# Retention heads: decay tables fetched ahead of the projections, and each head's scores issued ahead of the previous head's sums

## The chip, the cores and the metric

The kernel runs on one core of one Trainium2 chip, as one program with one launch. The metric is device time in microseconds, the median of several executions. All data is float32. The engines are TensorE (PE in the profile), VectorE (DVE), ScalarE (ACT), GpSimd (POOL) and SyncE (SP), which here only issues DMAs.

## The reference

Two blocks in a row act on 256 tokens of width 1024. The first block has an even layer (attention and a gated scan), an odd layer (retention), each followed by a feed-forward part; the second block has two layers with a gated delta rule and window attention. The change touches the odd layer's retention alone. It has 4 heads; queries and keys have 256 features each, values and gates 512. For the latent tokens:

```
p  = split_parts(h_lat @ w_in, ODD_PARTS)          # q, k, v, g
q_l = apply_rope(to_heads(p['q'], RET_HEADS), cos, sin)
k_l = apply_rope(to_heads(p['k'], RET_HEADS), cos, sin) * k_scale
v_l = to_heads(p['v'], RET_HEADS)
o_fw, _ = retention_chunked(q_l, k_l, v_l, log_g_fw, s_fw)
o_bw, _ = retention_chunked(flip(q_l), flip(k_l), flip(v_l), log_g_bw, s_bw)
y_lat = gated_head_norm(o_fw + flip(o_bw), p['g']) @ w_out
```

`s_fw` and `s_bw` come from the 256 context tokens. Retention is a product of queries and keys, weighted by a power of the head's decay that depends on the distance alone, times the values. `gated_head_norm` divides by the root mean square over the 512 values of a head and multiplies by silu of the gate.

## The kernel before

Every engine has its own hand-written order of instructions, and semaphores tie them together. Context and latent tokens (512 together) are kept as columns of `hT`. The kernel treats both directions and the context state of retention as one weighted score matrix for each head: 512 source tokens (four tiles of 128) by 256 target tokens. The weights are a table of 512 KB for each head, `const_ret[h]`, made on the host, and fetched into `r_D[:, h % 2]`, so there is room for two.

The odd layer runs in this order on TensorE: the norm; 8 blocks of query features, 8 of key features, 16 tiles of values and 8 of gates (`by_feature`, `by_token`, L775 and L763), whose weights come through a ring of two tiles of 2 MB that SyncE fills (L616) as TensorE releases them; then the four heads (L1277 to L1293); then transposes (`transposed`, L821) and the output projection (`down`, L805). ScalarE evicts each projection from a PSUM bank (`evac`, L1496), and VectorE sums modulation weights (L2106) in between and rotates queries and keys (L2632 to L2635).

For one head TensorE makes the scores into two PSUM banks, `mx[:, 0]` and `mx[:, 1]` (L1283: 8 matmuls of 256 columns), each bank signalled by `ret_s`. VectorE multiplies each bank by its half of the table into `r_P` (L2647, 2 instructions, signalled by `ret_p`). TensorE multiplies `r_P` with the values into banks `mx[:, 2]` and `mx[:, 3]` (L1291: 8 matmuls of 512 columns, signalled by `ret_o`). ScalarE squares and sums each of these banks (L1892, writing the squares to `r_junk`, which nobody reads), takes the logarithm and the exponential (L1550, L1551, signalled by `ret_rs`), and VectorE multiplies the bank, the reciprocal root and the gate (L2653, signalled by `ret_n`). Behind head h ScalarE waits for `ret_p` and issues the table of head h + 2 (`table`, L1868). Tables 0 and 1 are issued behind the last gate eviction (L1885, L1886).

The waits that hold the heads together: the scores of head h need both banks read (`ret_p`), the sums of head h need `r_P` written (`ret_p`) and their bank read (`ret_n`), VectorE's multiplication needs the table (`dtab_in`), the scores, and for h >= 2 the sums of head h - 2 (`ret_o`, since `r_P` has two halves).

`gate` is a buffer of 2 x 1024 columns that the norms use as scratch for squares and the reciprocal root (`n_sum`, `n_sq`, `n_rs`). `hT` holds the normed input, and from the transposes on (`roT`) the heads' outputs. `silu_tanh` and `exp_ln` load ScalarE's function tables (L1546, L1543).

Of the kernel before, what the change touches and what calls it, by code (L numbers as in the profile page):

```python
# [26 lines left out]
RET = 4  # L27
# [300 lines left out]
def need(eng, sem, value):  # L328

    if isinstance(value, int) and value <= 0:  # L330
        return
    eng.wait_ge(sem, value)
# [31 lines left out]
def first_then_second_block(nc, a, out):  # L364
# [3 lines left out]
    with ExitStack() as ctx:  # L368
        def sb(name, shape, dt=F32):
            return ctx.enter_context(nc.sbuf_tensor(name, shape, dt))  # L370
# [8 lines left out]
        gate = sb("gate", [P, 2, D])  # L379
# [16 lines left out]
        def view(at, *shape):  # L396
            n = int(np.prod(shape))
            assert at + n <= ARENA, (at, shape)
            v = arena[:, at:at + n]
            if len(shape) == 1:  # L400
                return v
            names = "abcd"[:len(shape)]
            return v.rearrange(f"p ({' '.join(names)}) -> p {' '.join(names)}", **dict(zip(names, shape)))
# [57 lines left out]
        hflat = hT[:, :, :].rearrange("p a b -> p (a b)")  # L461
# [33 lines left out]

        rv, rg, rk, rq = view(0, 4, 2048), view(8192, 2, 2048), view(12288, 8, 512), view(16384, 8, 256)
        r_t = view(18432, 2, 2, 256)
        r_P, r_D, r_junk = view(19456, 2, 4, 256), view(21504, 2, 4, 256), gate[:, 0, 0:512]

        dnf = view(0, 24, 256)  # L500
        sqk, s_v = view(6144, 2, 1152), view(8448, 2, 128)
# [193 lines left out]
        def _(pe):  # L695
# [39 lines left out]
            def bank():  # L735

                n = job.next()
                if pl.before[n] is not None:
                    emptied(pl.before[n] + 1, pl.who[pl.before[n]])
                return acc[:, pl.bank[n], :]  # L740

            def done(stage, n):

                emptied(pl.own[name_of(stage)][n - 1] + 1, pl.who[pl.own[name_of(stage)][n - 1]])
# [137 lines left out]
            def attention(base, units, fill):  # L882

                n = len(units)
                for u in range(n + 3):
                    if u < n:
                        q, k, blocks, v = units[u]
                        since(pe, att_m, base, u - 1)
                        nc.tensor.matmul(mx[:, u % 2, 0:P * blocks], q, k, start=True, stop=True).then_inc(att_s, 1)  # L889
                    fill(u)  # L890
                    if 2 <= u <= n + 1:
                        o, blocks = u - 2, units[u - 2][2]
                        pe.wait_ge(att_p, base + o + 1)
                        since(pe, att_pt, base, o)
                        for j in range(blocks):
                            ins = nc.tensor.transpose(mx[:, 2, P * j:P * (j + 1)], att_S[o % 3][:, P * j:P * (j + 1)], ident)
                        ins.then_inc(att_t, 1)
                    if u >= 3:
                        o, (_, _, blocks, v) = u - 3, units[u - 3]
                        pe.wait_ge(att_pt, base + o + 1)  # L900
                        since(pe, att_d, base, o)
                        for j in range(blocks):
                            ins = nc.tensor.matmul(mx[:, 3, HD * (o % 8):HD * (o % 8 + 1)],
                                                   att_PT[o % 2][:, P * j:P * (j + 1)], v[j],
                                                   start=j == 0, stop=j == blocks - 1)
                        ins.then_inc(att_o, 1)
# [21 lines left out]
            for i in BOTH:  # L928
                pe.wait_ge(qk_ready, i + 1)
                b = bank()  # L930
# [3 lines left out]
                b = bank()  # L934
# [84 lines left out]
            for slot in range(SLOTS):  # L1019
# [24 lines left out]
                if 3 <= slot < UNITS + 3:  # L1044
                    o, (_, _, blocks, v) = slot - 3, units[slot - 3]
                    pe.wait_ge(att_pt, o + 1)
                    since(pe, att_d, 0, o)
                    for j in range(blocks):
                        ins = nc.tensor.matmul(mx[:, 3, HD * (o % 8):HD * (o % 8 + 1)], ePT[o % 2][:, P * j:P * (j + 1)], v[j],
                                               start=j == 0, stop=j == blocks - 1)  # L1050
                    ins.then_inc(att_o, 1)
# [222 lines left out]
                by_token(tok, 512, where="odd")  # L1274
            pe.wait_ge(mod_c, len(MOD_GROUPS))
            done("ret_v", 16)
            for h in range(RET):  # L1277
                pe.wait_ge(ret_rope, h + 1)
                for s2 in range(2):
                    need(pe, ret_p, 2 * h - 1 + s2)  # L1280
                    for s in (2 * s2, 2 * s2 + 1):
                        for k in range(2):
                            ins = nc.tensor.matmul(mx[:, s2, 256 * (s % 2):256 * (s % 2) + 256],  # L1283
                                                   rk[:, 2 * h + k, P * s:P * (s + 1)], rq[:, 2 * h + k, :],
                                                   start=k == 0, stop=k == 1)
                    ins.then_inc(ret_s, 1)
                pe.wait_ge(ret_p, 2 * h + 2)
                for t in range(2):
                    need(pe, ret_n, 2 * h - 1 + t)
                    for s in range(4):  # L1290
                        ins = nc.tensor.matmul(mx[:, 2 + t, :], r_P[:, h % 2, s, P * t:P * (t + 1)],  # L1291
                                               rv[:, s, 512 * h:512 * (h + 1)], start=s == 0, stop=s == 3)
                    ins.then_inc(ret_o, 1)  # L1293
# [11 lines left out]
            for l in range(DEPTH2):  # L1305
# [12 lines left out]
                for i in range(2):  # L1318
                    pe.wait_ge(qk_ready, l * 2 + (NT + i + 1))
                    for j2 in range(2):  # L1320
                        b = bank()
# [4 lines left out]
                    b = bank()  # L1326
# [133 lines left out]
        def _(act):  # L1460
# [73 lines left out]
            def mod_after(where):  # L1534

                job_ = own.next()
                if job_ - 1 in MOD_SUM_AFTER.get(where, ()):
                    mod_turn()
                if job_ in MOD_SUM_AFTER.get(where, ()):
                    mod_sum()  # L1540

            def exp_ln():
                nc.scalar.preload_act_table_set(EXP_LN)  # L1543
# [323 lines left out]
            def table(h):  # L1867
                act.dma_start(r_D[:, h % 2], a["const_ret"][h]).then_inc(dtab_in[h % 2], 16)  # L1868

            own.n = 0  # L1870
            for f in range(8):
                evac(rq[:, f, :], 256)
# [8 lines left out]
            for c in range(4):  # L1881
                for t in range(2):
                    evac(rg[:, t, 512 * c:512 * (c + 1)], 512, ACT.Silu)
                    mod_after("odd")
            table(0)  # L1885
            table(1)  # L1886
            exp_ln()
            for h in range(RET):
                for t in range(2):
# [175 lines left out]
        def _(dve):  # L2065
# [5 lines left out]
            def name_of(stage):  # L2071

                return stage if layer[0] is None else f"{stage}@{layer[0]}"

            def job_done(name, n):

                dve.wait_ge(acc_a, pl.emptied("A", pl.own[name_of(name)][n - 1] + 1))
# [550 lines left out]
            for h in range(RET):  # L2628
# [8 lines left out]
                        link(ins)  # L2637
                ins.then_inc(ret_rope, 1)
                dve.wait_ge(ret_rope, h + 1)
            job_done("ret_g", 8)  # L2640
            for h in range(RET):
                dve.wait_ge(dtab_in[h % 2], 16 * (h // 2 + 1))
                if h >= 2:
                    dve.wait_ge(ret_o, 2 * (h - 1))
                for s2 in range(2):
                    dve.wait_ge(ret_s, 2 * h + s2 + 1)
                    V.tensor_tensor(r_P[:, h % 2, 2 * s2:2 * s2 + 2, :], mx[:, s2, :].rearrange("p (s t) -> p s t", s=2),  # L2647
                                    r_D[:, h % 2, 2 * s2:2 * s2 + 2, :], ALU.mult).then_inc(ret_p, 1)
                for t in range(2):
                    n = 2 * h + t  # L2650
                    dve.wait_ge(ret_rs, n + 1)
                    g = rg[:, t, 512 * h:512 * (h + 1)]
                    V.scalar_tensor_tensor(g, mx[:, 2 + t, :], st[:, 408 + n:409 + n], g,  # L2653
                                           ALU.mult, ALU.mult).then_inc(ret_n, 1)
# [15 lines left out]
            for l in range(DEPTH2):  # L2670
# [155 lines left out]
                for n in range(4):  # L2826
                    h, t = n // 2, n % 2
# [31 lines left out]
```

## Time and profile before

| | |
|---|---|
| median of 3 runs | 2884.79 us |
| lowest, highest | 2884.76, 2913.66 us |
| the profiled execution's own time | 2885.55 us |
| its span, first to last instruction | 2883.4 us |
| mean granted TensorE clock | 0.969 |
| TensorE busy | 2720.8 us, 94% |
| VectorE busy | 1542.3 us, 53% |
| ScalarE busy | 669.5 us, 23% |

The span is what the trace covers, and the time of an execution lies 2.15 us above it. Busy shares are averages over all stages. The profile shows each float32 matmul call as two records, so "x16" is eight calls of the source. A granted clock of 1.00 is 2.4 GHz and 0.50 is 1.2 GHz.

### The profile page before, as it was taken

The numbers are of one execution on the slowest core, as the hardware profiler recorded it, in microseconds if no ns is written. First come the engines' busy times: TensorE is split into PE (matmuls) and PEld (weight loads), VectorE is DVE, ScalarE is ACT, GpSimd is POOL, SyncE is SP. The second block draws the span as 40 slices with busy tenths as digits, with TensorE's granted clock in tenths as the row PEclk, the third lists the DMA queues.
The fourth block names the chain that finished last, engine by engine and source line by source line (L and its number), as shares of the span: only waits on it lengthen the run. The fifth ranks groups of instructions, "written<-read, shape, count | busy, mean of one in ns | idle before, by whom it ended". The sixth has DMA issues, their size and how long they took to land.

```text
span 2883.4 us, 36232 instructions
## 1 busy us (share of the span) xinstructions
PE 2720.8 (94%) x14426; PEld 2050.3 (71%) x14426; DVE 1542.3 (53%) x3100; ACT 669.5 (23%) x1727; POOL 0.2 (0%) x4
## 2 busy tenths in 40 slices
PE   6899988999999999899999999989998999998999
PEld 2445555888887444589977756668996864775999
DVE  4856555755775521136745554425773654443775
ACT  3134322111102100212111351222311144222330
POOL 0000000000000000000000000000000000000000
PEclk9998889999999999999999999999999999999999
DMA  7530012555475844145634221124553322113554
GB/s 291 200 94 23 34 55 88 175 161 171 174 282 199 304 165 163 59 130 164 181 131 151 97 88 59 59 88 130 164 182 127 134 88 88 59 59 101 154 168 134
DMA packets 336164, 387.36 MB, mean 134 GB/s; under 512 B 10988, under 2 KB 265084, under 8 KB 323452
## 3 DMA queue, kind: packets, MB, share of 16 engines
q1 hardware_dynamic: 333260, 378.15, 39.9%
q10 hardware_dynamic: 2736, 6.89, 0.7%
q8 instruction: 115, 1.88, 0.3%
q14 instruction: 53, 0.43, 0.0%
HBM read 383.96 MB, written 1.05 MB: 134 GB/s over the span
## 4 chain that ended last, share of the span: by engine, by line
PE 86%; DVE 6%; DMA 3%; ACT 3%; issue 2%; ACTq 0%; SPq 0%; DVEq 0%
PE acc L724 24%; PE acc L763 12%; PE acc L775 11%; PE mx L724 10%; PE acc L789 8%; PE acc L1031 2%; PE acc L1016 2%; PE acc L805 2%; PE mx L1409 1%; PE mx L1398 1%; PE mx L1407 1%; DVE arena L2106 1%; PE mx L889 1%; PE mx L1291 1%; PE acc L821 1%
## 5 line engine op out<-in xcount | busy, mean ns | idle before, releaser
L763 PE MATMUL acc<-ring,hT 128*128 128x512 f32 (+2 forms) x1152 | 407.6, 515 | 19.3 <-DMA ring<-in_even_w_in 9.5
L763 PEld LDWEIGHTS acc<-ring,hT 128*128 128x128 f32 x1152 | 197.9, 194 | 226.2 <-issue 207.6
L724 PE MATMUL acc<-arena 128*128 128x128 f32 (+1 forms) x2056 | 322.6, 299 | 2.1 <-ACT gate L1817 0.8
L775 PE MATMUL acc<-hT,ring 128*128 128x256 f32 (+1 forms) x1280 | 311.5, 407 | 12.8 <-DMA ring<-in_w_in 8.1
L775 PEld LDWEIGHTS acc<-hT,ring 128*128 128x128 f32 x1280 | 246.9, 193 | 76.5 <-issue 33.8
L724 PEld LDWEIGHTS acc<-arena 128*128 128x128 f32 x2056 | 282.8, 192 | 16.1 <-ACT gate L1817 1.4
L2106 DVE SCALAR_TENSOR_TENSOR arena<-mod_w,vcols,arena 128x2048 f32<-128x2048 f32 x98 | 228.4, 2348 | 110.4 <-DMA mod_w<-in_w_ada 100.9
L789 PE MATMUL acc<-ring,hT 128*128 128x512 f32 x512 | 258.0, 625 | 1.1 <-ACT hT L1496 1.1
L724 PE MATMUL acc<-hT,ring 128*128 128x128 f32 (+1 forms) x1208 | 194.9, 311 | 12.1 <-ACT hT L1586 12.0
L2453 DVE TENSOR_TENSOR arena<-ring 128x512 f32<-128x512 f32 (+1 forms) x136 | 91.6, 674 | 192.6 <-PE acc L724 184.7
L724 PEld LDWEIGHTS acc<-hT,ring 128*128 128x128 f32 x1208 | 171.6, 197 | 26.5 <-issue 11.8
L724 PE MATMUL acc<-arena,ring 128*128 128x128 f32 (+1 forms) x1160 | 182.4, 300 | 1.9 <-DVE x L2594 1.9
L724 PEld LDWEIGHTS acc<-arena,ring 128*128 128x128 f32 x1160 | 159.7, 192 | 10.4 <-DVE x L2594 2.7
L1496 ACT ACTIVATE arena<-acc 128x512 f32<-128x512 f32 (+2 forms) x136 | 69.8, 527 | 414.2 <-PE acc L763 293.4
L789 PEld LDWEIGHTS acc<-ring,hT 128*128 128x128 f32 x512 | 91.4, 196 | 89.7 <-issue 84.4
L724 PE MATMUL mx<-hT,ring 128*128 128x128 f32 (+1 forms) x928 | 151.0, 307 | 0.0
L724 PE MATMUL mx<-arena,ring 128*128 128x128 f32 (+1 forms) x928 | 148.5, 302 | 0.0
L724 PEld LDWEIGHTS mx<-hT,ring 128*128 128x128 f32 x928 | 132.5, 196 | 6.5
L724 PEld LDWEIGHTS mx<-arena,ring 128*128 128x128 f32 x928 | 128.7, 191 | 9.0 <-issue 3.4
L724 PE MATMUL acc<-hT,arena 128*128 128x128 f32 (+1 forms) x760 | 124.7, 307 | 0.0
L724 PEld LDWEIGHTS acc<-hT,arena 128*128 128x128 f32 x760 | 108.3, 191 | 6.0
L1031 PE MATMUL acc<-hT,ring 128*128 128x512 f32 x192 | 99.7, 659 | 0.0
(355 smaller groups left out, 3441.0 us busy)
## 6 DMA issues: line engine op xcount, KB each, us to landing
ring<-in_w_in SPq DMA_DIRECT2D x28, 2048.0 KB
mod_w<-in_w_ada SPq DMA_DIRECT2D x48, 1024.0 KB, 5.9
ring<-in_ffn_w_in SPq DMA_DIRECT2D x88, 512.0 KB
ring<-in_w_up SPq DMA_DIRECT2D x88, 512.0 KB
mod_w<-in_mod_w SPq DMA_DIRECT2D x40, 1024.0 KB, 5.0
ring<-in_odd_w_in SPq DMA_DIRECT2D x12, 2048.0 KB
ring<-in_ffn_w_out SPq DMA_DIRECT2D x16, 1024.0 KB
ring<-in_w_down SPq DMA_DIRECT2D x16, 1024.0 KB
```

Of the source, the lines that this page charges most:

```text
L724: ins = nc.tensor.matmul(out, w[:, k, :], h[:, k, :], start=start and k == 0, stop=stop and k == n - 1, skip_group_check=more)
L763: ins = nc.tensor.matmul(b[:, 0:width], src[:, k, P * i:P * (i + 1)], w[:, k, :], start=k == 0, stop=k == KD - 1)
L775: ins = nc.tensor.matmul(b[:, 0:hi - lo], w[:, k, P * f:P * (f + 1)], hT[:, k, lo:hi], start=k == 0, stop=k == KD - 1)
L789: ins = nc.tensor.matmul(filling.b, src[:, k, P * i:P * (i + 1)], filling.w[:, k, :], start=k == 0, stop=k == KD - 1)
L805: ins = nc.tensor.matmul(b[:, 0:width], w[:, k, P * f:P * (f + 1)], src[:, at + k, :], start=at + k == 0, stop=at + k == sum(groups) - 1)
L821: ins = nc.tensor.transpose(b[:, at:at + P], src[:, i, P * (k + q):P * (k + q + 1)], ident)
L889: nc.tensor.matmul(mx[:, u % 2, 0:P * blocks], q, k, start=True, stop=True).then_inc(att_s, 1)
L1016: ins = nc.tensor.matmul(b, w[:, k, P * f:P * (f + 1)], hT[:, first + k, :], start=k == 0, stop=k == 3)
L1031: ins = nc.tensor.matmul(hb, hw[:, kk, P * j:P * (j + 1)], hT[:, kk, :], start=kk == 0, stop=kk == KD - 1)
L1496: ins = nc.scalar.activation(dst, src, func, **kw)
L2106: ins = V.scalar_tensor_tensor(acc_, mod_w[:, i % 2, :], vcols[:, at:at + 1], acc_, ALU.mult, ALU.add)
L2453: V.tensor_tensor(s3, a11, a10, ALU.subtract)
```

## The change

Tables 0 and 1 are issued on ScalarE's queue before the first eviction of the odd layer's projections. The tables' place moves from the arena, where modulation sums live until the heads begin, to all of `gate`; `r_junk` moves from `gate` to the first 512 columns of `hT`. On TensorE the scores of head h + 1 are issued ahead of the sums of head h, and on VectorE the multiplication of head h + 1 ahead of the norm products of head h.

```diff
-        r_P, r_D, r_junk = view(19456, 2, 4, 256), view(21504, 2, 4, 256), gate[:, 0, 0:512]
+        r_P, r_junk = view(19456, 2, 4, 256), hflat[:, 0:512]
+        r_D = gate[:, :, :].rearrange("p a b -> p (a b)").rearrange("p (h s t) -> p h s t", h=2, s=4)
...
-            for h in range(RET):
+            def ret_scores(h):
                 pe.wait_ge(ret_rope, h + 1)
                 for s2 in range(2):
                     need(pe, ret_p, 2 * h - 1 + s2)
...
                     ins.then_inc(ret_s, 1)
+
+            ret_scores(0)
+            for h in range(RET):
+                if h + 1 < RET:
+                    ret_scores(h + 1)
                 pe.wait_ge(ret_p, 2 * h + 2)
...
             def table(h):
                 act.dma_start(r_D[:, h % 2], a["const_ret"][h]).then_inc(dtab_in[h % 2], 16)
 
+            table(0)
+            table(1)
             own.n = 0
...
-            table(0)
-            table(1)
             exp_ln()
...
-            job_done("ret_g", 8)
-            for h in range(RET):
+            def weighted(h):
                 dve.wait_ge(dtab_in[h % 2], 16 * (h // 2 + 1))
                 if h >= 2:
                     dve.wait_ge(ret_o, 2 * (h - 1))
...
+
+            job_done("ret_g", 8)
+            weighted(0)
+            for h in range(RET):
+                if h + 1 < RET:
+                    weighted(h + 1)
                 for t in range(2):
                     n = 2 * h + t
                     dve.wait_ge(ret_rs, n + 1)
```

## Rows read from the trace of the kernel before

**Rows 1.** The page: busy times, and the chain by engine.

```profile
PE 2720.8 (94%) x14426; PEld 2050.3 (71%) x14426; DVE 1542.3 (53%) x3100; ACT 669.5 (23%) x1727; POOL 0.2 (0%) x4
...
PE 86%; DVE 6%; DMA 3%; ACT 3%; issue 2%; ACTq 0%; SPq 0%; DVEq 0%
```

**Rows 2.** The chain of waits, retention heads: start us, length us, what.

```profile
1161.25 5.21 DMA arena<-in_const_ret
...
1166.65 1.30 DVE arena L2647 x2
...
1168.00 8.83 PE mx L1291 x16
1176.83 3.47 PE mx L1283 x16
...
1180.32 0.70 DVE arena L2647
...
1181.06 7.13 PE mx L1291 x16
...
1203.81 7.15 PE mx L1291 x16
...
1213.07 4.52 PE acc L821 x24
```

**Rows 3.** Timeline at the start of head 0: start us, us, what, idle before.

```profile
1161.53 3.72 PE L1283 MATMUL mx<-arena 128*128 128x256 f32 x16 [0.32 <-ACT modc L1522]
```

**Rows 4.** Windows: engines' busy us, then granted clock, DMA share, GB/s.

```profile
1165.00:1168.00 3.00, 0.26 (x3) 0.00 (x1) 1.29 (x2) 0.00 (x0) 0.00 (x0) 1.00 1.04 393
1169.40:1172.80 3.40, 3.40 (x6) 1.32 (x5) 0.00 (x0) 0.00 (x0) 0.00 (x0) 0.50 0.41 129
1173.00:1204.00 31.00, 28.65 (x90) 16.56 (x89) 8.37 (x12) 7.11 (x24) 0.00 (x0) 1.00 0.11 34
...
1213.80:1217.20 3.40, 3.40 (x19) 3.40 (x18) 0.00 (x0) 2.57 (x5) 0.00 (x0) 0.50 0.00 0
...
908.00:920.00 12.00, 12.00 (x52) 10.36 (x52) 5.30 (x4) 4.10 (x9) 0.00 (x0) 0.92 0.00 0
```

**Rows 5.** The line that issues the tables (L1868): time from issue to landing.

```profile
DMA to landing us min/median/max: 3.5/4.4/7.0
```

**Rows 6.** SyncE's queue: issues merged, from the first to the last.

```profile
895.11 26.51 SPq L616 DMA_DIRECT2D ring<-in_odd_w_in  x2
921.67 15.24 SPq L598 DMA_DIRECT2D mod_w<-in_w_ada  x4
...
1160.86 72.93 SPq L616 DMA_DIRECT2D ring<-in_odd_w_out  x2
```

**Rows 7.** Timeline, ScalarE at the projections' start, and at the tables' old place.

```profile
909.69 1.28 ACT L1546 ACT_TABLE_LOAD   x1
910.98 0.38 ACT L1496 ACTIVATE arena<-acc 128x256 f32<-128x256 f32 x1
914.26 0.38 ACT L1496 ACTIVATE arena<-acc 128x256 f32<-128x256 f32 x1 [2.90 <-PE acc L775]
...
1161.25 0.34 ACTq L1868 DMA_DIRECT2D arena<-in_const_ret  x1
```

**Rows 8.** Timeline behind the sums of head 0: table 2, and the norm product.

```profile
1177.91 0.34 ACTq L1868 DMA_DIRECT2D arena<-in_const_ret  x1
1178.14 0.75 DVE L2653 SCALAR_TENSOR_TENSOR arena<-mx,st,arena 128x512 f32<-128x512 f32 x1 [2.68 <-ACT st L1551]
```

**Rows 9.** The chain of waits, layers 0 and 1 of the second block.

```profile
1621.81 3.49 PE acc L763 x32
...
1905.51 3.69 PE acc L821 x16
...
2318.58 3.49 PE acc L763 x32
...
2598.79 2.95 PE acc L821 x16
```

## The prediction

> **What bounds the kernel now.** I began with the page. TensorE is busy for 94% of the span and holds 86% of the chain that ended last [rows 1], so an edit is worth what it takes off TensorE's own timeline. The change touches one stage, the retention heads. In the chain of waits of that stage [rows 2] the reader should see four heads, each a block of score products (3.47 us) and a block of weighted sums (7.13 us), and three kinds of lost time. First, in head 0, the chain leaves TensorE for a DMA: the decay table is issued at 1161.25 and takes 5.21 us. The timeline [rows 3] says that the scores of head 0 start at 1161.53, so they end at 1161.53 + 3.47 = 1165.00, and the sums start at 1168.00: **3.00 us** idle. Second, the sums of head 0 take 8.83 us where every later head takes 7.13 us, **1.70 us** more. The windows [rows 4] say why: from 1165 to 1168 TensorE is nearly idle, and from 1169.4 to 1172.8 its granted clock is 0.50, the 1.2 GHz level, against 1.00 (2.4 GHz) before the idle time. Third, in each later head the scores end at 1176.83 + 3.47 = 1180.30 and the sums start at 1181.06, after VectorE's second multiplication by the table (0.70): **0.76 us**, three times; these short gaps leave the clock at 1.00 [rows 4].
>
> **The change, part by part.**
>
> *Tables early.* Tables 0 and 1 are issued ahead of the projections' evictions instead of behind them. VectorE then never waits for them, as some 250 us lie between. Without the new order head 0 would still wait the ordinary 0.76, so this part removes 3.00 - 0.76 = 2.24 us, and with the long idle time the slow clock behind it, 1.70: **3.94 us**.
>
> What it costs. The two issues move to where ScalarE has loaded its function table, at 910.98, ahead of its first eviction [rows 7]. At their old place the first took 0.34 and the next began 0.37 after it, so the eviction comes under 1 us late. The next eviction waits 2.90 us for TensorE anyway, and TensorE fills four banks in turn, so it asks for the first again only four blocks (some 14 us) on. If that cover were gone the cost would be that one microsecond. On the DMA engines, the two transfers (1 MB together) fall into a stretch with nothing in it: from 908 to 920 their share is 0.00 [rows 4]. SyncE issued its first projection load of [rows 6] at 895.11, and then waited until 921.2 to issue the second, because the ring had to be released; nothing of it is queued behind ScalarE. Issued at about 911 with the longest landing seen (7.0 us, [rows 5]) they are in by 918.4 and meet nothing. Cost: zero, and at worst, were they to collide with a weight load that TensorE waits for, the 2.7 us that 1.05 MB takes at the 393 GB/s of [rows 4].
>
> The Trainium skill speaks against this part (DMA: Bandwidth & Descriptors, "Issuing engines are not separate DMA queues"): loads started by ScalarE run on the same 16 DMA engines as SyncE's and interleave with them. Read that way, an early fetch only moves 1 MB into another load's time. The trace bears the rule out at the old place, where tables and an output weight tile are in flight together and the first table takes 5.21 us against 3.5 for the undisturbed ones; at the new place there is no other load, so the sum stays.
>
> *New places.* The decay tables move into the norm's scratch, and the square's throw-away output into the start of hT. Both are the same SBUF accesses at other addresses: zero. The norm's next writer of that scratch comes after all heads, and hT's last reader, the last gate projection, is ahead of the heads on TensorE. No wait is added by either.
>
> *Scores one head ahead.* TensorE's order becomes S0, S1, W0, S2, W1, S3, W2, W3 (S scores, W sums). VectorE multiplies head h+1 ahead of the norm products of head h. Nothing is added, the same instructions run. Step by step from 1161.53, with 3.47 and 7.13: S0 ends at 1165.00. S1's first half needs bank 0, read by VectorE after S0's first half (1163.27 + 0.70 = 1164.0): free. Its second half, due 1166.74, needs the second multiplication: 1165.00 + 0.76 = 1165.8: free. S1 ends at 1168.47, and W0 has had its factors since 1165.8. W0 to 1175.60, S2 to 1179.07, W1 to 1186.20, S3 to 1189.67, W2 to 1196.80, W3 to **1203.93**. The banks of the sums are free in time too: the norm product is done some 2.1 us after a half of the sums (1210.96 to 1213.07 for the last), so the first bank is free for W3 at 1196.80 - 3.57 + 2.1 = 1195.3, 1.5 us ahead, and the second at 1198.9 for 1200.4; W1 and W2 have more. In the trace W3 ends at 1203.81 + 7.15 = 1210.96. The new order takes 4 x 0.76 = 3.04 us, the tables 3.94, together 6.98; the two end points give 7.03. I take **7.0 us**.
>
> The new order's cover for tables 2 and 3: ScalarE issues a table 1.08 us after a head's sums (1177.91 against the end at 1176.83, [rows 8]), so table 2 at 1176.7 and table 3 at 1187.3. Before, table 2 was wanted when head 2's first scores were done, from about 1189.8, 12 us after its issue. Now table 2 must be in before S3 wants bank 0 at 1186.2, less 0.7: 8.8 us. Table 3 must be in early enough for its two multiplications (1.35) and the norm product of head 2 queued behind them (0.75) to be done by W3 at 1196.8: 7.4 us. The undisturbed landings are the shortest, 3.5 [rows 5], and SyncE issues nothing from 1160.86 until 1233.8 [rows 6]. Zero, with 4 us to spare.
>
> *What is late next.* After W3 the old tail stays: square, logarithm, exponential, norm product, then the transposes, 1210.96 to 1213.07, 2.1 us. ScalarE and VectorE have nothing else there. The stages after it are paced by TensorE, their loads released by TensorE's progress, so they shift as a whole. The second slow stretch, 1213.8 to 1217.2 [rows 4], follows this tail and I leave it as it is. From the profiled execution's own time: 2885.55 - 7.0 = 2878.5 (its span 2876.4). That execution lies 0.76 above the median of the runs; from the median: 2884.79 - 7.0 = **2877.8**.
>
> **The rivals.**
>
> *Clock, this stage.* The first slow stretch might come all the same, or the one behind the tail might go, each worth up to 1.7 us: 2879.5 or 2876.1. Against the first: TensorE has no gap left in the 42 us. Against the second: the gap of 2.1 us is unchanged. A chance of 0.03 and 0.05.
>
> *Clock, all that follows.* Every later gap comes 7 us earlier, and whether the clock falls at a gap can go either way. A bound from rows: both layers of the second block run the same program, yet from the last value projection to the transposes behind the delta heads one takes 1905.51 - 1621.81 = 283.7 us and the other 2598.79 - 2318.58 = 280.2 [rows 9]. I put the whole 3.5 on this: 2874.3 to 2881.3. Chance 0.07. The Trainium skill (TensorE: Matmul & The Clock Gate, "What's actually happening") says the same of one kernel from run to run, that how many slow matmuls it meets varies with where its work lies against a monitor that does not restart with the kernel; the gap between profiled and median time here, 0.76 us, is smaller than one fall.
>
> *Only the tables help.* If a wait that I read as free holds S(h+1) or W(h) back, 3.94 of the 7.0 is left: 2880.9. It would be VectorE's norm product of head h standing behind head h+1's multiplication; by the sum above it is ready 1.5 us ahead. Chance 0.03.
>
> *Slower: the norm behind a late table.* Place: VectorE's queue, where head 2's norm products stand behind head 3's multiplication and so behind table 3, and head 1's behind table 2. Before, a late table held back only its own head. Each microsecond of landing beyond 7.4 (table 3) and 8.8 (table 2) is lost. The gain is used up where (L - 7.4) + (L - 8.8) = 7.0, from L = 11.6 us; at 13 us the loss is 9.8 and the time 2887.6. For it: one table did take 7.0. Against it: that one shared the engines with a 2 MB load and a second table. Chance 0.02.
>
> *The change does nothing.* The waits removed are on the chain by the trace, so 2884.8 would need a new one of just that size. Chance 0.01.
>
> **How the numbers follow.** Forecast 0.79; the rest as above. The forecast with the cases of the clock and of the tables alone runs from 2874.3 to 2881.3; with 0.76 between two executions of the kernel on either side I give 2874.0 to 2881.8. A measurement of this kernel can tell about 1%, 29 us, from no change; no case above reaches that on either side: faster by over 1% 0.01, within 0.97, slower 0.02.
>
> **What would show it.** In the trace after: two table issues near 911 and landed by 918; no DMA in the chain of the retention stage; TensorE without idle time from the first score to the last sum, some 42.4 us; four sums of 7.13 each and clock 1.00 throughout; tables 2 and 3 landing in about 3.5; the output projection starting 7.0 us earlier against the last gate projection. I am wrong if a gap of over 0.5 us stands before a sum (then VectorE's order), or if the stage is 7 us shorter and the whole is not (then the clock in the later stages).

## The result and the profile after

Over 20 executions each, the changed kernel has a median of 2877.97 us (2868.37 to 2904.65) and the kernel before 2884.99 us (2876.93 to 2913.91). The ratio of the times is **0.9947, 95% interval [0.9922, 0.9973]**. The profiled execution of the change took 2877.97 us, its span 2875.8, against 2885.55 and 2883.4. So the median is where I put it (2877.8), and the ratio, which is not that of the medians (0.9976), gives twice the gain: 15 us, and even its near end (0.27%, 7.8 us) lies past my 7.0. Both numbers can't be read without one fact: executions of this program fall into two groups, one up to 2892 us and one from 2903 us, and 4 of the 20 before and 1 of the 20 after lie in the upper one. Where these 30 us come from is looked for among the experiments.

On the page of the changed kernel, busy times and the chain by engine answer to [rows 1]. Nothing is to be seen there but 2 us less of TensorE:

```profile
PE 2718.8 (95%) x14426; PEld 2052.4 (71%) x14426; DVE 1543.4 (54%) x3100; ACT 670.0 (23%) x1727; POOL 0.2 (0%) x4
...
PE 86%; DVE 6%; DMA 3%; ACT 3%; issue 2%; ACTq 0%; SPq 0%; DVEq 0%
```

The chain of waits of the changed kernel over the heads (start us, length us, what; L1284 are the scores, L1297 the sums) answers to [rows 2] and [rows 3]:

```profile
1159.27 7.17 PE mx L1284 x32
1166.44 6.87 PE mx L1297 x16
1173.31 3.45 PE mx L1284 x16
1176.76 6.87 PE mx L1297 x16
1183.62 3.45 PE mx L1284 x16
1187.08 13.75 PE mx L1297 x32
...
1202.94 0.67 PE acc L822 x4
...
1207.71 17.32 PE acc L806 x79
```

No DMA and no VectorE is left between the first score and the last sum: two score blocks, then sums and scores in turn, then two sums. The heads take 1200.83 - 1159.27 = **41.56 us**, against 1210.96 - 1161.53 = 49.43. A block of sums takes 6.87 us here and took 7.13 behind each gap, a difference that I had not in the sum. The weight loads (PEld) show what a gap costs beyond its idle time. Here is the first load for the sums of head 1, before and after:

```profile
1181.06 0.30 PEld L1291 LDWEIGHTS mx<-arena 128*128 128x128 f32 x2 [1.19 <-DVE arena L2647]
```

```profile
1176.38 0.41 PEld L1297 LDWEIGHTS mx<-arena 128*128 128x128 f32 x2
```

Before, it started with the block, when VectorE was done (1181.06). After, it started 0.38 us ahead of the block (1176.76), while TensorE was still at the scores.

From the last sums to the output projection it is 1207.71 - 1200.83 = 6.88 us, against 8.27.

The windows of the changed kernel (busy us by engine, granted clock, DMA share, GB/s) answer to [rows 4]. The clock stays at 1.00 through all heads and behind them, and from 908 to 920 us the DMA engines, which stood empty before, are busy for 0.23 of the time:

```profile
1159.30:1201.00 41.70, 41.51 (x128) 24.20 (x128) 10.60 (x15) 9.66 (x30) 0.00 (x0) 1.00 0.24 76
...
1203.00:1208.00 5.00, 3.94 (x33) 3.71 (x34) 0.00 (x0) 4.03 (x8) 0.00 (x0) 1.00 0.00 0
908.00:920.00 12.00, 12.00 (x58) 10.55 (x56) 3.26 (x2) 2.46 (x5) 0.00 (x0) 1.00 0.23 83
```

The timeline of ScalarE at the tables' new place answers to [rows 7], and the line that issues them to [rows 5]:

```profile
906.68 0.33 ACTq L1874 DMA_DIRECT2D gate<-in_const_ret  x1
906.74 0.49 ACT L1591 ACTIVATE hT<-hT,mb 128x256 f32<-128x256 f32 x1
907.05 0.45 ACTq L1874 DMA_DIRECT2D gate<-in_const_ret  x1
907.14 0.49 ACT L1592 ACTIVATE hT<-hT,mb 128x256 f32<-128x256 f32 x1
907.65 1.28 ACT L1552 ACT_TABLE_LOAD   x1
908.94 0.38 ACT L1502 ACTIVATE arena<-acc 128x256 f32<-128x256 f32 x1
```

```profile
DMA to landing us min/median/max: 3.4/3.5/4.3
```

The issues go out at 906.68 us beside ScalarE's last shifts of the norm, not behind its function table. The first eviction comes 908.94 - 902.18 = 6.76 us after the first projection matmul, and 910.98 - 904.23 = 6.75 before: not even the one microsecond was charged. No table takes over 4.3 us, where one took 7.0.

### The profile page after: what moved, and what is told of

Read it like the earlier page. It is cut to its first block, busy times and chain, and to the rows that moved or that the text cites. A ratio compares the mean times of both kernels' runs of the same rounds, so it can differ in the third digit from the quotient of the medians.

```text
span 2875.8 us, 36232 instructions
## 1 busy us (share of the span) xinstructions
PE 2718.8 (95%) x14426; PEld 2052.4 (71%) x14426; DVE 1543.4 (54%) x3100; ACT 670.0 (23%) x1727; POOL 0.2 (0%) x4
## 3 DMA queue, kind: packets, MB, share of 16 engines
HBM read 383.96 MB, written 1.05 MB: 134 GB/s over the span
## 4 chain that ended last, share of the span: by engine, by line
PE 86%; DVE 6%; DMA 3%; ACT 3%; issue 2%; ACTq 0%; SPq 0%; DVEq 0%
PE acc L725 24%; PE acc L764 12%; PE acc L776 11%; PE mx L725 10%; PE acc L790 8%; PE acc L1032 2%; PE acc L1017 2%; PE acc L806 2%; PE mx L1415 1%; PE mx L1404 1%; PE mx L1413 1%; DVE arena L2112 1%; PE mx L890 1%; PE mx L1297 1%; PE acc L822 1%
## 5 line engine op out<-in xcount | busy, mean ns | idle before, releaser
L776 PE MATMUL acc<-hT,ring 128*128 128x256 f32 (+1 forms) x1280 | 311.3, 406 | 12.5 <-DMA ring<-in_w_in 7.8
L725 PEld LDWEIGHTS acc<-arena,ring 128*128 128x128 f32 x1160 | 159.7, 192 | 10.3 <-DVE x L2600 2.6
```

The source lines that it names most:

```text
L725: ins = nc.tensor.matmul(out, w[:, k, :], h[:, k, :], start=start and k == 0, stop=stop and k == n - 1, skip_group_check=more)
L776: ins = nc.tensor.matmul(b[:, 0:hi - lo], w[:, k, P * f:P * (f + 1)], hT[:, k, lo:hi], start=k == 0, stop=k == KD - 1)
```

## The experiments

In each, "heads" is the time from the first score to the end of the last sums, and "tail" from there to the output projection, both read from the trace.

**The kernel before, against itself.** No edit.

> The kernel before, unchanged, against itself: what a comparison of this kernel shows when nothing differs. Theory A (the change is worth 7 to 9 us and the rest of any difference is the spread from run to run): single runs between 2877 and 2914 us, a ratio of 1.000 give or take 0.002 to 0.003, and in the trace the heads, from the first score product to the end of the last sums, again take 49.4 us, and 8.3 us more to the output projection, unless the slow clock moves. Rival B (something else of the change, upstream or downstream of the heads, is worth 8 us or more): then this run's stages outside the heads agree with those of before within 1 us.

Median 2883.21 us over 12 executions, ratio 0.9991 [0.9941, 1.0041]. The chain of this copy at the heads and behind them:

```profile
1155.77 5.05 DMA arena<-in_const_ret
...
1162.36 8.82 PE mx L1291 x16
...
1205.33 0.70 ACT gate L1892 x2
...
1208.11 4.03 ACT hT L1496 x8
...
1212.19 13.00 PE acc L805 x59
```

Heads 1205.31 - 1156.05 = 49.26 us, tail 6.88 us. So the heads' time is firm, the slow clock behind the table's wait too (8.82 again), but the slow stretch of [rows 4] behind the heads isn't the kernel's: the same program had it in one execution and not in the other. The stages outside differ by up to 2.5 us between the two traces, mostly in steps near 1.7 us. So with nothing changed they do not agree within the 1 us that the rival wanted, and stage differences of this size can't be put down to the change.

**Early tables alone.** The early issues and the new places, the old order:

```diff
+            table(0)
+            table(1)
             own.n = 0
...
-            table(0)
-            table(1)
```

> Only the early fetch and the new places; the old order of the heads. By the prediction's sum this alone takes 2.24 us of idle time and 1.70 us of slow clock: heads 49.4 - 3.9 = 45.5 us, four gaps of 0.76 left, no DMA in the chain, clock 1.00 through all heads. The whole 3.9 us faster, 2881 us. Rival (the new order is what counts, the table's wait would have been hidden): heads 48 us or more.

Chain of this kernel, head 0 and the first sums of head 1:

```profile
1159.90 3.73 PE mx L1284 x16
1163.63 0.02 issue
1163.65 0.70 DVE arena L2648
1164.36 0.04 issue
1164.40 7.13 PE mx L1292 x16
...
1175.77 7.13 PE mx L1292 x16
```

Heads 45.76 us, and 45.77 in a second trace (an execution of 2876.23 us). That is 3.4 to 3.7 less than before, where I had put 3.94: the step holds. Median 2877.93, ratio 0.9985 [0.9935, 1.0034].

**The new order alone.** Tables late and in their old place:

```diff
+            ret_scores(0)
+            for h in range(RET):
+                if h + 1 < RET:
+                    ret_scores(h + 1)
...
+            weighted(0)
+            for h in range(RET):
+                if h + 1 < RET:
+                    weighted(h + 1)
```

> Only the new order; tables 0 and 1 issued behind the last gate eviction, in the old places. Table 0 lands at about the same time as before (5.2 us after its issue), so head 0's first multiplication ends about 6.5 us after the first score starts, and the second score block waits for it: I expect an idle time of about 2.5 us before the second block of scores, then no further gaps. If the slow clock follows that gap again, heads 41.6 + 2.5 + 1.7 = 45.8 us; if it doesn't, 44.1 us. Whole: 3.6 to 5.3 us faster. Rival: the order does nothing without early tables: 49.4 us.

> The new order with late tables, one look (4 of its 12 executions lay in the upper group). Heads 45.5 us again. If in the upper group: the same stage as for the kernel before, by theory A; a stage at the heads by theory C.

This kernel was traced twice (executions of 2878.13 and 2882.46 us), and the two traces show both cases of the expectation: heads 45.53 and 44.03 us. The windows of the first, then of the second, over the second block of scores:

```profile
1161.00:1163.20 2.20, 0.16 (x2) 0.04 (x1) 0.85 (x2) 0.00 (x0) 0.00 (x0) 1.00 1.03 390
1163.20:1168.00 4.80, 4.80 (x15) 3.93 (x16) 1.13 (x2) 0.00 (x0) 0.00 (x0) 0.64 0.73 238
```

```profile
1163.00:1166.00 3.00, 1.01 (x5) 0.94 (x6) 1.29 (x2) 0.00 (x0) 0.00 (x0) 1.00 1.04 381
1166.00:1170.00 4.00, 4.00 (x17) 2.97 (x16) 1.38 (x2) 0.00 (x0) 0.00 (x0) 1.00 0.56 178
```

TensorE stood idle for 2.04 us in the first and 2.23 us in the second, with the same work behind it. Behind the shorter wait the clock fell and the block of scores took 5.38 us; behind the longer one it did not, and the block took 3.69. So the parts don't add up by themselves (3.9 and 3.0): the order alone saves 3.8 or 5.3, since its second block of scores needs only the first of the two multiplications, and so also shortens the table's wait (2.74 us before). Median 2879.76, ratio 0.9994 [0.9952, 1.0036].

**The change again.**

> The changed kernel once more. Theory A: heads 41.6 us again, as in its first trace (49.4 before, 7.9 less: the 7.0 of the prediction and 0.26 us for each restart of TensorE behind a gap, which a block of sums took as 7.13 and now takes as 6.87). The tail from the last sums to the output projection took 6.9 us against 8.3; if that is the place of the slow clock and not the change, it may come out at either value here. The median 7 to 9 us below before. Rival B: a further gain outside the heads, then the stages before 1150 us or after the output projection are shorter again by several us, in the same places as in the first trace.

Heads 41.56 and tail 6.88 us, to the hundredth what the first trace had. Median 2874.52 over 12, ratio 0.9928 [0.9889, 0.9967]: a gain of 21 us, again more than the heads give.

**TensorE kept busy in the table's wait.** The kernel before, with this ahead of the sums of head 0:

```diff
+                if h == 0:
+                    for j in range(3):
+                        nc.tensor.matmul(mx[:, 2, 0:512], rk[:, j, 0:P], rv[:, 0, 0:512], start=True, stop=True)
                 pe.wait_ge(ret_p, 2 * h + 2)
```

> The kernel before with 3 extra matmuls of 128x512 (2.6 us, their result is overwritten) on TensorE between the scores and the sums of head 0, where it waited 3.0 us for the decay table. Theory (the 1.70 us by which head 0's sums were longer is the slow clock behind that wait, and the clock keeps its level if TensorE works): the sums of head 0 take 7.1 us or less instead of 8.8, start at the same distance from the first scores as before (6.4 to 6.5 us), and the heads take 47.6 us instead of 49.4. Rival (the long first sums come from elsewhere, reads of values just written or the DMA landing beside them): 8.8 us again.

Chain of this kernel (L1294 are the sums):

```profile
1158.01 5.43 DMA arena<-in_const_ret
...
1164.98 7.13 PE mx L1294 x16
1172.11 3.47 PE mx L1283 x16
```

One execution, 2885.33 us. The table is as late as ever (sums start 6.69 us after the first score, 6.47 before), the first sums take 7.13 us, and the heads 47.95. In all five traces of the kernel before and of its variants that leave this wait empty (2.5 to 3.2 us idle), they take 8.6 to 8.8. So the 1.70 us were the clock, which kept its level where TensorE had work.

**Tables 2 and 3 made late.** The changed kernel with n further loads into unused space ahead of each (n is 2 and then 6; the waits for these loads are left out here):

```diff
...
+                    for j in range(n):
+                        act.dma_start(junk[j], a["const_ret"][h + 2]).then_inc(junk_in, 16)
                     table(h + 2)
```

> The changed kernel with two further loads of 512 KB (into unused space) issued ahead of table 2 and of table 3, so that each lands about 6 us after the old issue time instead of 3.5. By the prediction's bound (7.4 us for table 3, 8.8 for table 2) nothing is lost: heads 41.6 us, no gap. Rival (there is less room than the sum says): a gap ahead of the fourth block of scores or the last sums.

> The same with six further loads ahead of each, landing about 11.5 us after the old issue time. By the bound (11.5 - 7.4) + (11.5 - 8.8) = 6.8 us are lost: heads about 48.4 us, and up to 3.4 more if the clock falls behind the gaps. The gaps stand ahead of the second half of head 3's scores or ahead of the last sums. Rival (the new order hides more than that, for instance since the norm products aren't what TensorE waits for): heads under 45 us.

Each was executed once (2875.84 and 2885.31 us), so the traces decide. With two further loads the tables were ready 6.0 and 6.1 us after the old issue time, and the heads took 41.56 us: nothing was lost. With six, 47.26 us. The timeline of the latter (L1288 scores, L1301 sums, L2661 VectorE's multiplication, L1910 the further loads):

```profile
1173.05 1.78 ACTq L1910 DMA_DIRECT2D mod_w<-in_const_ret  x4
...
1183.43 1.78 ACTq L1910 DMA_DIRECT2D mod_w<-in_const_ret  x4
1184.20 1.29 DVE L2661 TENSOR_TENSOR arena<-mx,gate 128x512 f32<-128x512 f32 x2 [10.16 <-DMA gate<-in_const_ret]
1185.04 5.13 PE L1288 MATMUL mx<-arena 128*128 128x256 f32 x16 [2.76 <-DVE arena L2661]
...
1195.97 1.29 DVE L2661 TENSOR_TENSOR arena<-mx,gate 128x512 f32<-128x512 f32 x2 [9.16 <-DMA gate<-in_const_ret]
...
1198.06 7.10 PE L1301 MATMUL mx<-arena 128*128 128x512 f32 x16 [1.02 <-DVE arena L2673]
```

Table 2 was ready 1184.17 - 1173.05 = 11.1 us after the old issue time and cost 2.76 us (bound: 11.1 - 8.8 = 2.3), then the clock fell, and the scores took 5.13 where they take 3.45 without a gap. Table 3 was ready after 1195.94 - 1183.43 = 12.5 us, which by the bound alone costs 5.1, but TensorE was already 2.76 + 1.68 = 4.4 us late, and 1.02 was left. The two bounds hold to within half a microsecond. That they add up, as I had written for the slower rival, does not hold: the later one counts only for what the earlier delay hasn't used.

**Transposes in two parts.** A step beyond the change:

```diff
-            pe.wait_ge(ret_n, 2 * RET)
+            pe.wait_ge(ret_n, 2 * RET - 2)
             stage("ret_oT")
-            transposed(rg, (0, 1), 2)
+            transposed(rg, (0, 1), 2, last=6)
+            pe.wait_ge(ret_n, 2 * RET)
+            transposed(rg, (0, 1), 2, first=6)
```

> The changed kernel with the transposes in two parts: those of heads 0 to 2 are issued when the norm products of heads 0 to 2 are done, those of head 3 behind the last norm product as before. Four of the six early ones have a free bank and can run in the 2.1 us in which TensorE waited for the last norm product; ScalarE evicts them only behind its own last exponential, at its pace of about 0.5 us each. I expect the time from the last sums to the output projection to fall from 6.9 us to about 5, heads 41.6 as before: the whole 1.5 to 2 us under the change, 2873 us. Rival (ScalarE's eight evictions, 4.0 us in a row behind its exponential, are the bound): from 1.3 us behind the sums the evictions take 4.0, so 5.3 to 5.5, of 6.9, a gain of at most 1.5.

> The split transposes again, beside the changed kernel on the same chip. Its tail took 5.23 us against 6.88, so 1.65 us under the changed kernel in the lower group; that is less than the spread of a median of 11 (about 1.5 us), so the medians may come in either order, and the trace's tail of 5.2 us decides.

Chain of this kernel behind the last sums:

```profile
1201.39 0.70 ACT hT L1900 x2
...
1202.64 3.91 ACT hT L1504 x8
...
1206.60 18.61 PE acc L806 x85
```

Heads 41.56, tail 5.23 us in both traces, with ScalarE's eight evictions as the bound, as the rival said. Medians 2874.53 (11 executions, ratio to before 0.9957 [0.9935, 0.9978]) and 2875.98 (12, 0.9961 [0.9931, 0.9991]; one of the 12 in the upper group). It is the quickest of the kernels by its stages, 1.65 us under the change.

**Looking for the 30 us.**

> The kernel before, one look. The executions of this kernel fall into two groups, most between 2872 and 2891 us and about a quarter between 2903 and 2917; of the changed kernel's 32 executions so far 2 lie in the upper group. This look is to find, if it falls in the upper group, the stage that holds the 30 us. Theory A (the slow clock, in a stage ahead of or behind the heads, that the change doesn't touch): one stage outside the heads is longer by some 30 us at a granted clock of 0.50, the heads 49.3 us as ever. Theory C (the wait for the decay table starts it): the extra time begins at or right behind the heads. In the lower group: stages as in the first trace but for steps of 1.7 us.

> As the look before it: one execution in four falls in the upper group; if so, its stage is to be named, and the heads are to take 49.3 us.

> Early tables with the old order, one look (4 of its 12 executions lay in the upper group). Heads 45.8 us again. If in the upper group: the same stage as for the kernel before, by theory A; by theory C it could not be there, since no wait for a table is left.

The first of these executions of the kernel before took 2877.51 us, the second **2914.35 us**, early tables alone 2876.23. The second lies in the upper group; it is the only traced execution that does. Stage by stage it differs from the first by 30.2 us in one place: the attention of the second block's first layer, 109.71 us from its first score to the first matmul behind its transposes and eight blocks of the output projection, against 79.47; no other stage differs by over 3.4. Its heads took 49.36 us. Its windows there, then those of the first trace of before in the same stage:

```profile
1629.00:1690.00 61.00, 61.00 (x127) 31.55 (x126) 23.76 (x104) 19.06 (x76) 0.00 (x0) 0.50 0.12 43
1694.00:1718.00 24.00, 24.00 (x104) 14.14 (x104) 16.56 (x62) 11.11 (x42) 0.00 (x0) 1.00 0.00 1
```

```profile
1636.00:1692.00 56.00, 56.00 (x233) 32.90 (x233) 40.34 (x168) 27.70 (x116) 0.00 (x0) 1.00 0.11 38
```

Both of these enter the stage with a fall of the clock. In the usual trace it is over after some 8 us; here it stays at 0.50 for over 60 us, and comes back within the same stage. The fall alone doesn't do it: of the 34 entries into the two attention stages of the second block in all 17 traces, 29 show a granted clock below 1.00 over the first 4 us, and only this one stays low for over 12 us. The chain of the slow trace shows one attention step after the other at 3.26 us each, all on TensorE, which didn't wait for the softmax there (1.75 in the usual one):

```profile
1640.19 2.00 PE acc L789 x2
1642.19 0.21 PE mx L896
1642.41 0.32 PE mx L903 x2
1642.73 0.72 PE mx L889 x2
1643.45 2.00 PE acc L789 x2
```

That is theory A: a stage 400 us behind the heads, which the change doesn't touch. That the other executions of the upper group have the same cause is not shown by a trace, only made likely by their distance: the group's mean lies 29.2 us above the lower one's for the kernel before, and 29.1 for the change. Theory C, that the table's wait starts it, has against it that early tables alone, without that wait, had 4 of 12 executions in the upper group.

**The count once more.**

> The changed kernel against before once more, to count the upper group. So far: before and its copy 22 of 86 executions near 2903 to 2917 us, the changed kernel 2 of 32, its variants with split tail or more table loads 0 of 13. If the change keeps executions out of the long slow-clock state in the first attention of the second block (109.7 us there against 79 to 83), again at most 1 of some 11, against 2 to 4 for before. If the count was chance (theory A: the heads' 7.9 us and nothing else belong to the change), 2 to 4 of 11. Lower groups 6 to 8 us apart either way.

Now 3 of the change's 12 executions and 3 of 29 of before lie in the upper group, the ratio is 0.9989 [0.9957, 1.0021], and the medians are 2879.80 and 2885.80. In all: 25 of 115 executions of before and its copies, 5 of 44 of the change. A difference of that size comes about by chance once in ten (exact test, one side). But the share also differs between the lots in which kernels ran side by side: before and its copies had 4 of 20, 16 of 47, 1 of 16 and 3 of 29 there. Compared within lots, chance gives it once in seven. With the variants that contain the change (further loads, split transposes: 1 of 25) it is once in twelve. Early tables alone and the new order alone together had 8 of 26, 8 of 24 of them in the lot of 16 of 47, so nothing suggests that either part alone lowers it. So the smaller number in the upper group, which went into 0.9947 and 0.9928, is not shown to be the change's doing, nor shown to be chance.

**Fillers packed at the start of the attention.**

```diff
-                attention(l * 32 + 32, units, lambda u: fill(1, hT, LAT) if u < 32 else None)
+                attention(l * 32 + 32, units, lambda u: fill(2 if u < 8 else 1, hT, LAT) if u < 24 else None)
```

> The kernel before with the fillers of both attention stages of the second block packed more densely at the start: two in each of the first 8 steps, one in the next 16, none in the last 8, instead of one in each of 32. Theory (the upper group is the slow clock keeping itself in the attention, whose steps leave TensorE waiting on the softmax when it is slow, started by the fall at the stage's entry): with more TensorE work in the first steps the state is left early, so no execution, or at most 1 of 11, in the upper group; the lower group within 3 us of before. Rival (the fillers don't matter for it): 2 to 4 of 11 in the upper group.

All 12 executions lie between 2893.64 and 2901.91 (median 2897.01, ratio 1.0020 [0.9993, 1.0048]): none 30 us higher, but none near the usual times of before either. Both attention stages are longer, 89.4 and 91.9 us against 80.1 and 80.5 in the first trace of before. The fall at the entry is still there (0.63 over the first 4 us of the first stage), and a further, longer one has come in the last steps, which have no filler left. Windows of this kernel:

```profile
1666.00:1674.00 8.00, 8.00 (x33) 4.36 (x32) 5.79 (x21) 3.80 (x16) 0.00 (x0) 1.00 0.01 2
...
1690.00:1698.00 8.00, 7.67 (x25) 5.24 (x24) 5.10 (x21) 3.62 (x14) 0.00 (x0) 0.50 0.01 2
```

My theory of it (a denser start lets the slow clock be left early, at no cost) is refuted in the second half: the price is 11 us on the median. The first half is not shown. No execution at +30 us among 12 comes about by chance once in three, since before had only 3 of 29 there in this lot. The premise fails too, that TensorE waits on the softmax when the clock is low: in the slow trace the profile has it busy for 61.00 of 61.00 us.

## Why the prediction was right or wrong

**Head 0's wait and its slow clock (3.94).** Right: 3.4 to 3.7 alone, and the filled wait shows that 1.70 of it was the clock. The rest of the difference is a misreading: I let the scores of head 0 take 3.47 us, where [rows 3] has 3.72. They end at 1161.53 + 3.72 = 1165.25, TensorE is idle for 2.75 us and not 3.00, and the term is 3.69.

**The gaps of the four heads (3.04).** Right in mechanism, and the mis-sized term of the sum. I took the idle time only, 0.76 us. Taking the gap away also made the sums 0.26 us shorter, 6.87 for 7.13. The traces fit the first weight load as its cause, which starts with the block behind a gap and ahead of it without one, but no run changed the load alone. With early tables in both, the order is worth 45.77 - 41.56 = 4.21 us, four times 1.05. The whole stage: 49.2 to 49.4 before in four traces, 41.56 in three of the change, **7.6 to 7.9 us** for my 7.0.

**The tables' new place.** Right, and cheaper still, zero. The DMA engines had been empty there, and the tables landed in 3.4 to 4.3 us. The Trainium skill's rule (DMA: Bandwidth & Descriptors, "Issuing engines are not separate DMA queues") had nothing to act on here; at the old place the traces agree with it, with 5.05 us for the first table in the kernel's copy against 3.4 for the quickest one.

**VectorE's new order.** Right. No gap stands before any block, and with tables at 11 to 12.5 us it fails within half a microsecond of where the bound says. The step "the gain is used up where (L - 7.4) + (L - 8.8) = 7.0" was wrong: the two don't add up.

**The tail.** I left its slow clock in place. Of the 15 traces with the old transposes 5 have it (tail 8.2 to 8.4 us) and 10 don't (6.9), and the kernel before, the change and variants are among both. It belongs to the execution. In the first pair of traces it made the difference over heads and tail 9.3 us.

**The step that failed: "The forecast with the cases of the clock and of the tables alone runs from 2874.3 to 2881.3; with 0.76 between two executions ..."** (Added as written, this gives 2873.5 to 2882.1, and not my 2874.0 to 2881.8.) I took the spread from two layers of one trace (3.5 us) and from one pair of executions (0.76). The lower group alone spreads over 20 us, and the upper one lies 30 us above it. The sign stood in the times before, 2913.66 as one of three, and I did not ask which stage it was. A figure that compares all times carries the share of such executions: in the first 20 the plain means are 2888.43 and 2878.11, 10.3 us apart, of which 6.2 lie between the lower groups and the rest is 4 against 1 in the upper one. That is a ratio of 0.9964, and what 0.9947 has beyond it lies within its interval. Pooled, the lower groups are 2882.9 (standard error 0.5) and 2876.4 (0.7), 6.5 us apart (6.2, 7.6 and 5.7 in the three lots), and the medians 2885.2 and 2878.0, 7.2 apart. The size of the gain was right to one microsecond, by the heads (7.6 to 7.9) and by these figures; the range wasn't a range for what a comparison of 20 executions can show. That the first median came within 0.2 us of 2877.8 is luck: the next two of the same kernel are 2874.52 and 2879.80.

**Still open:** what decides whether the clock comes back at the attention's start, whether all executions of the upper group are of this kind, and whether the change has any part in the smaller number. The 44 executions of the change are too few to settle the last.

## What to carry to other kernels

A gap on TensorE costs more than its idle time: here 0.26 us each time it starts again, and 1.7 us where a gap of 2.0 to 3.2 us let the clock fall, so pricing the wait alone undervalues filling it. Before a change of a quarter of a percent is judged, look at the spread of the executions and find the stage that holds the outlying ones; stage times out of the traces (41.56 each time) resolve what 20 whole times don't. And when two late transfers hold up one chain one after the other, let the first delay count against the second, as here (2.76 and then 1.02 us, not 6.8 together).

## What the runs showed of the hardware that I had not expected

In one program the granted clock fell behind a gap of 2.04 us in one execution (0.64 in the mean over the next 4.8 us) and stayed at 1.00 behind 2.23 us in another. Behind the 2.5 to 3.2 us of the kernel before it fell in five traces of five, and behind its gaps of 0.76 us in none. In the second block's attention it stayed at the 1.2 GHz level for over 60 us in one execution, with the profile's TensorE busy throughout, and made a stage of 79.5 us one of 109.7. The Trainium skill (TensorE: Matmul & The Clock Gate, "Seeing it yourself") has, in a caution that clock events in traces can be unreliable, a clock seen stuck low for 50 us and more. This trace agrees in the duration, not in the level that the page names, and here the steps themselves took longer (3.26 us for 1.75), so it is no error of the record.
